# Two-pass up-projections on four PSUM banks, modulation sums on a new schedule, constants in two loads, and a few reorderings

## The reference, cut to what matters

```python
sh1, sc1, g1, sh2, sc2, g2 = split(silu(c) @ w_ada + b_ada, 6)      # w_ada: 2048 x 12288
h_l = rms_norm(x, norm1_w) * (1 + sc1) + sh1                        # h_c: the same for ctx
... = split(h_l @ w_in, IN_OFFSETS)                                 # gated linear + differential attention
gates = sigmoid(h_l @ w_gate + b_gate)
x = x + g1 * ((g_a * (ya @ w_proj_gla) + g_b * (yb @ w_proj_diff)) @ w_out)
h2 = rms_norm(x, norm2_w) * (1 + sc2) + sh2
u = h2 @ w_up                                                       # 2048 x 11264
u = sum(up[:, j:j + T] * conv_w[j] for j in range(3)) + conv_b      # a 3-tap conv over tokens
x = x + g2 * ((silu(gate) * val) @ w_down)                          # gate, val = halves of u
```

## Time and profile before

| | |
|---|---|
| median of 3 runs | 2309.18 us |
| the profiled execution | 2309.0 us, its span 2307.2 us |
| TensorE matmuls busy | 2235.6 us, 97% |
| TensorE weight loads busy (beside the matmuls) | 2007.1 us, 87% |
| VectorE busy | 1486.6 us, 64% |
| ScalarE busy | 1026.8 us, 45% |
| mean granted TensorE clock | 0.994 of full speed |

### The profile page before, as it was taken

One profiled execution on the slowest core, in us unless ns is written; L12 is line 12 of the kernel. 1 busy time (PEld: TensorE's weight loads), 2 busy tenths in 40 slices (PEclk: granted clock), 3 DMA queues, 4 the chain that ended last, 5 costly groups with the idle time before them and its releaser, 6 DMA issues.

```text
span 2307.2 us, 37356 instructions
## 1 busy us (share of the span) xinstructions
PE 2235.6 (97%) x15465; PEld 2007.1 (87%) x15465; DVE 1486.6 (64%) x2116; ACT 1026.8 (45%) x1410; POOL 52.7 (2%) x68
## 2 busy tenths in 40 slices
PE   5899999999999999999999999999999999999998
PEld 2577877999988999779999988999978998999986
DVE  2347866487576579777888854566675644576664
ACT  3134343354555633344444433444454434454443
POOL 3000000021000000000000000000000000000000
PEclk9999999999999999999999999999999999999999
DMA  9956766454444578866777655555555566534454
GB/s 364 379 163 208 250 191 216 132 148 137 139 135 129 186 248 287 284 236 203 229 245 258 226 190 192 183 183 183 183 178 194 171 189 200 171 129 137 129 199 148
DMA packets 249738, 458.75 MB, mean 199 GB/s; under 512 B 18995, under 2 KB 43889, under 8 KB 248160
## 3 DMA queue, kind: packets, MB, share of 16 engines
q1 hardware_dynamic: 246496, 442.47, 59.4%
q0 software_dynamic: 2496, 9.69, 1.2%
q10 hardware_dynamic: 576, 4.19, 0.5%
HBM read 454.20 MB, written 2.10 MB: 198 GB/s over the span
## 4 chain that ended last, share of the span: by engine, by line
PE 83%; DVE 7%; DMA 3%; DVEq 2%; ACT 2%; issue 1%; SPq 1%; ACTq 0%; POOLq 0%; POOL 0%
PE psum L660 74%; DVE fast L1919 2%; PE psum L637 2%; DVE sbuf L1973 1%; DMA sbuf<-in_w_ada 1%; DMA sbuf<-in_w_up 1%; ACT fast L1335 1%; PE psum L1169 1%; DVEq L1972 1%; PE psum L916 1%; PE psum L971 1%; DVE fast L1941 1%; PE psum L731 1%; PE psum L1199 1%; PE psum L990 1%
## 5 line engine op out<-in xcount | busy, mean ns | idle before, releaser
L660 PE MATMUL psum<-fast,fast 128*128 128x256 f32 (+1 forms) x13424 | 2028.1, 312 | 14.6 <-DVE fast L1919 12.4
L660 PEld LDWEIGHTS psum<-fast,fast 128*128 128x128 f32 x13424 | 1845.0, 190 | 186.6 <-issue 41.3
L1919 DVE TENSOR_TENSOR fast<-sbuf,fast 128x1024 fp32r<-128x1024 f32 (+5 forms) x685 | 784.1, 1153 | 661.9 <-ACT fast L1335 654.1
L1335 ACT ACTIVATE fast<-sbuf 128x1024 fp32r<-128x1024 f32 (+4 forms) x689 | 681.9, 997 | 1024.0 <-PE psum L660 882.8
L1973 DVE SCALAR_TENSOR_TENSOR sbuf<-sbuf,sbuf 128x512 f32<-128x512 f32 x210 | 157.9, 752 | 20.2 <-DMA sbuf<-in_w_ada 2.7
L1335 ACT ACTIVATE sbuf<-psum 128x512 f32<-128x512 f32 (+4 forms) x193 | 86.1, 469 | 93.6 <-PE psum L660 48.2
L637 PE MATMUL psum<-sbuf,sbuf 128*128 128x128 f32 (+2 forms) x349 | 59.2, 286 | 19.3 <-DMA sbuf<-in_consts 10.1
L637 PEld LDWEIGHTS psum<-sbuf,sbuf 128*128 128x128 f32 (+2 forms) x349 | 43.3, 147 | 30.1 <-DMA sbuf<-in_consts 10.1
L1941 DVE TENSOR_TENSOR fast<-sbuf,fast 128x512 fp32r<-128x512 f32 (+1 forms) x61 | 53.4, 876 | 4.9 <-issue 0.4
L1694 ACT ACTIVATE sbuf<-psum,sbuf 128x256 f32<-128x256 f32 x88 | 44.1, 551 | 0.0
L2354 DVE SCALAR_TENSOR_TENSOR sbuf<-psum,sbuf,sbuf 128x255 f32<-128x255 f32 x88 | 38.5, 479 | 3.3
(11 more groups left out here) (265 smaller groups left out, 956.5 us busy)
## 6 DMA issues: line engine op xcount, KB each, us to landing
sbuf<-in_w_ada SPq DMA_DIRECT2D x192, 512.0 KB, 5.1
sbuf<-in_w_up SPq DMA_DIRECT2D x176, 512.0 KB, 4.6
sbuf<-in_w_in SPq DMA_DIRECT2D x154, 512.0 KB, 3.7
sbuf<-in_w_down SPq DMA_DIRECT2D x88, 512.0 KB, 3.9
sbuf<-in_w_gate SPq DMA_DIRECT2D x64, 512.0 KB, 3.6
sbuf<-in_w_out SPq DMA_DIRECT2D x64, 512.0 KB, 4.8
sbuf<-in_w_proj_gla SPq DMA_DIRECT2D x16, 512.0 KB, 4.7
sbuf<-in_w_proj_diff SPq DMA_DIRECT2D x16, 512.0 KB, 6.2
```

The costliest lines, as they stand in the source:

```text
L660: last = mm(out, lhsT, rhs, start=first and key not in opened, stop=end, skip_group_check=True)
L1335: return A(out, in_, ACT.Copy, scale=scale)
L1919: last = tt(lo, raw, hi.bitcast(F32), ALU.subtract)
```

## The change

Up-projections: hi times [hi | lo] of the activations in one matmul of 512 columns (a whole bank), then lo times hi in 256 columns into its first half. A job takes four banks (gate 0 to 3, value 4 to 7). ScalarE copies the second halves out, VectorE adds them onto the first halves in PSUM, then `centre` and `taps` go on as before. Sums: block 16 and 17 move beside w_gate, 18 and 19 keep 16 sums beside pg, pd and out, 20 to 23 get fixed steps beside w_up. Constants: only `ones` and `rowsel` (132 columns) are loaded at the start, the other constants and w_a_up after block 7. The merges of a pd job move into the steps of the next job; in key_norms the side work goes ahead of rest and sums; some roundings go behind the copies out of PSUM; the rest after out3 goes behind row_variance. The compression stage's semaphores are joined under two names, with the same waits.

```diff
-          ("cmprel", 32), ("cmpmask", 32), ("levels", 7 * P), ("rowsel", 4),
+CONSTS = [("ident", 128), ("ones", 128), ("rowsel", 4), ("blk64", 128), ...
+NCONST0 = CCOL["blk64"][0]
+UP_SUMS = [16 * i + r for i in range(6) for r in (6, 7, 9, 12, 13, 15)][:32]
+for _i in range(KF // 4):
+    BANKS[f"ug{_i}"], BANKS[f"uv{_i}"] = (0, 1, 2, 3), (4, 5, 6, 7)
...
-        for n in range(8):
-            self.add(f"gate{n}", panel("w_gate", 512 * n, 512))
+        self.beside([(f"gate{n}", panel("w_gate", 512 * n, 512)) for n in range(8)], ada, (16, 17),
+                    [1 + 15 * n // 4 for n in range(16)], {})
...
-                    + [... "w_out" ...], ada, range(16, 20), 15, 8)
+                    + [... "w_out" ...], ada, (18, 19),
+                    [6 + 2 * n for n in range(8)] + [31 + 3 * n for n in range(8)], {4: 16, 8: 17, 24: 18, 56: 19})
-        self.beside(ups[:KFA // 2], ada, range(20, 24), 5, 2, 14)
+        self.beside(ups[:KFA // 2], ada, range(20, 24), UP_SUMS, {36: 20, 52: 21, 68: 22, 100: 23})
...  # POOL
-            pool.dma_start(cst[:, P:], dram["consts"][:, P:NCONST1]).then_inc(S("consts_loaded"), 16)
+            pool.dma_start(cst[:, P:NCONST0], dram["consts"][:, P:NCONST0]).then_inc(S("consts_loaded"), 16)
...
+            pool.wait_ge(S("plain_multiplied"), st.done("ada7")[1])
...  # the eight w_a_up loads
+            pool.dma_start(cst[:, NCONST0:], dram["consts"][:, NCONST0:NCONST1]).then_inc(S("consts_loaded"), 16)
...  # TensorE
+            def wide(first, act):
+                def products(k, hi, lo):
+                    return [(2 * b, cut(bank(b), 2, T),
+                             [(hi[:, m * P:(m + 1) * P], act[:, :, k, :]),
+                              (lo[:, m * P:(m + 1) * P], act[:, 0, k, :], bank(b, 0, T))])
+                            for m, b in enumerate(range(first, first + 4))]
...
-                    gemm(f"u{'gv'[v]}{i}", features(v, hL), ...)
+                    gemm(f"u{'gv'[v]}{i}", wide(4 * v, XR[:, 0, :, :, :]), ...)
...  # ScalarE, at step 8 (gate) and 0 (value) of 16; centre one step later
+            def copy_halves(s, i):
+                for b in range(2):
+                    copy(ftap[s][:, 2 * b:2 * b + 2, :], cut(banks(4 * s + 2 * b), 2, 2, T)[:, :, 1, :]
+                         ).then_inc(S("halves_copied"), 1)
...  # VectorE, same steps; taps one step later
+            def halves(s, i):
+                for b in range(2):
+                    dve.wait_ge(S("halves_copied"), 4 * i + 2 * s + b + 1)
+                    pair = cut(banks(4 * s + 2 * b), 2, 2, T)
+                    tt(pair[:, :, 0, :], pair[:, :, 0, :], ftap[s][:, 2 * b:2 * b + 2, :], ALU.add).then_inc(S("halves_added"), 1)
...
             for name in ("dk1", "dv0", "dv1"):
-                steps(name)
+                for g in st.job[name]:
+                    next(side, None)
+                    rest_chunk(st.nth[g] + 2)
+                    modulation(st.nth[g])
...
+            for n in range(4):
+                steps(f"pd{n}")
+                side = merges(n)
...
             row_variance(48, 4, ("x1_squared", 8))
+            rest_chunk(st.nth[st.job["out3"][-1]] + 2)
```

More of the change, by code:

```diff
@@ L249, in add, with beside @@
             self.counts[kind] += 1
-    def beside(self, jobs, ada, parts, num, den, first=0):
+    def beside(self, jobs, ada, parts, steps, folds=None):
         todo = [(a, i) for a in parts for i in range(len(ada[a]))]
-        at = {}
-        for n, x in enumerate(todo):
-            at.setdefault(first + n * num // den, []).append(x)
+        at, base = {}, self.counts[0]
+        for x, step in zip(todo, steps, strict=True):
+            at.setdefault(step, []).append(x)
+        for step, a in (folds or {}).items():
+            self.fold_at[base + step] = self.keep_at[base + step + 1] = a
         for n, (name, c) in enumerate((name, c) for name, chunks in jobs for c in chunks):
@@ L280, in before, with folded_before @@
             tiles += len(BANKS[job]) - 1
+    def folded_before(self, s):
+        return [a for step, a in self.fold_at.items() if a >= 20 and step < s]
     def landed(self, g):
@@ L1495, in _ @@
             for j in range(2):
[L1496 removed]
+                steps(f"dk{j}", j)
                 if j == 0:
@@ L2280, in _, with merges @@
                         ).then_inc(emptied, 1)
-            for n in range(4):
-                steps(f"pd{n}")
+            def merges(n):
                 for b in range(2):
```

111 lines of the change are left out of this document (68 added, 43 removed).

## The result

The changed kernel takes 2294.82 us, the median of 4 runs (2292.72 to 2296.4), against 2308.96 before on the same chip: ratio 0.9938, 95% interval 0.9925 to 0.9951. That is faster by 14.1 us, inside the stated range of 2268 to 2296, where 30.8 were forecast. The profiled execution took 2294.8 us, its span is 2292.6 (before 2307.2).

The account below looks back on a forecast made before the run. TensorE, busy 97% of the span, was taken to bound the kernel. From 2309.0 us, the terms -18.3 + 3.0 - 9.2 - 3.2 - 3.1 = -30.8 gave 2278.2 us, with a stated range of 2268 to 2296.

Parts of the forecast that it names:

- Step 1: w_up: one 512-column pass replaces two of 256, 346.4 ns a pair against 359.4, over 1408 pairs: -18.3 us.
- Step 2: First 96 chunks of w_up: added copies and adds make VectorE late, 0.5 us per group: +3.0 us, bounds 0 and 10.0.
- Rival A: First 96 chunks of w_up: VectorE sets the pace, nothing is left of 768 pairs' gain; 2285.2 us, chance 0.17.
- the last sentence of the prediction: Beside w_up: the forecast fails if VectorE is over 95% taken and TensorE's windows fall under 98%.
- Step 3: pd and out: sums moved away and merges spread remove TensorE's stops and low clock: -9.2 us, bounds -6 and -9.7.
- The sums beside w_gate: w_gate: the 16 sums moved there fit VectorE's free time and do not delay the attention: 0 us.
- Rival C: w_gate: the sums placed there delay the attention, 14 us exposed; 2292 us, chance 0.08.
- Step 4: Start: 1.21 MB of constants and w_a_up leave the stretch with saturated DMA: -3.2 us, bounds 0 and -4.5.
- Step 5: Key stage: key scaling ahead of rest and sums, and an earlier copy out of PSUM: -3.1 us, bounds 0 and -3.1.
- Rival B: w_up: time goes with columns, not with matmuls, so two passes gain 0; 2293.5 us, chance 0.07.

Follow-up runs that it names:

- the groups: The changed kernel with each w_up chunk doing its 8 passes of 512 columns first, then its 8 of 256: 2295.52 us, ratio 0.9940.
- merges_back: The changed kernel with both halves of a pd job's merges done at once after it, as before the change: 2301.52 us, ratio 0.9966.
- sums_back_beside_out: The changed kernel with the sums of blocks 16 and 17 back beside the projections and w_out, none beside w_gate: 2300.76 us, ratio 0.9966.

## Why the prediction was right and wrong

**Step 1, two passes for three (-18.3): the size of the term failed.** The two paces that it was built of were right, each among its like: 226.7 and 120.0 ns inside the groups. What the step overlooked is that it put them side by side: it added the pair up to 346.4 ns, and the pair took 353.3 in all of the last 80 chunks and much of the first 96. A change of size costs 10 ns on average between groups of eight; the alternation has two steady states, 353.3 and 346.7 ns a pair. The first gives 6.1 ns a pair (8.6 us in all), the second 12.7, nearly the forecast's 13.0. The last 80 chunks ran wholly in the slow state: 4.3 us gained where 8.3 were forecast. The earlier trace rows held a warning, that 512 columns took 226.6 in one place and 231.3 in another; I took the nearer row and left 231.3 as a bound. With it the step gives -11.7, still more than came. The price from the Trainium skill's "TensorE: Matmul & The Clock Gate", section "Back-to-back issue gap", gives 3.5 us for the step, nearer to what came, but not by its figures: it has 109.2 and 215.8 ns for the two sizes, and the groups ran at 120.0 and 226.7. That section also calls the formula the gap of a single matmul by itself, so the prediction stretched it when it set it against a stream.

**Step 2, VectorE (+3.0): direction right, size too small.** The step named the mechanism, lateness of rests and slots freed late, and put 0.5 us on each group. In the first 96 chunks the intervals between matmuls that are longer than their pace, other than at folds and at the first chunks, add up to 7.2 us in the changed kernel and to nothing in that with the sums spread: 7.2 us of stops, inside the stated bound of 10.0. Rival A's outcome came, that nothing is left of those 768 pairs (282.1 us with two passes, 281.8 with three). Its condition, no spare time on VectorE, did not: counted as the prediction counts it, VectorE was taken for 164.8 of 180 us (92%, before 87%), since each stop is made by one bad sequence and not by the mean. Of the two conditions in the last sentence of the prediction one came true: TensorE's windows beside w_up fell under 98% (76.85 us of 80 from 1160 to 1240, 96%), while VectorE stayed under 95%.

**Step 3, sums and merges (-9.2): right, -11.7,** of which 1.7 are two folds that only moved ahead of pd0, so -10.0. The sums brought most of it, the merges 2.9.

**The sums beside w_gate (0): wrong by 4.7 us,** 6.4 less the 1.7 of the two folds. The cover was counted from where exponentials end to where TensorE needs them, 4.1 us against 1.8. That was one step of sixteen, and sixteen steps don't have the same cover: where a sum stood in a step with a maximum, TensorE came to wait 0.3 to 1.5 us. Rival C named the mechanism with a chance of 0.08; its price of 14 us was three times too high. Putting the attention first brings back 2.4 of the 4.7; 1.6 of what is left are the two stops that remain, and why these remain was not looked into.

**Step 4, late constants (-3.2): right in sign, -5.4** in this pair of profiles, past the stated bound of -4.5; -4.2 in the middle of all profiles with late constants, which is inside it. In 20 to 60 us, with the DMA engines at 1.05 in both, TensorE was busy 31.1 us with the constants early and 35.3 late, at clock 1.00; behind it, to 125 us, the mean clock was 0.89 and 0.92. How much of what exceeds the 3.2 is the clock's, no run separates.

**Step 5, keys first (-3.1): right, -3.2** from gv0 to gq.

**Not in the prediction: downb, +3.3.** Nothing of the change touches it. But w_up now ends with ScalarE's and VectorE's last tap work a step later, and an order that had cost 1.7 us costs 2.6, after which the clock fell in this execution and in seven other profiles, but not in four. The forecast looked for stops only where the edits were.

In sum, by the table: 8.8 us are missing in w_up (4.8 and 4.0, from pace and stops, less the 2.5 that are won there without the passes), 6.4 from w_gate on, 3.3 in downb and 2.5 in the first w_down part and the second layer, against 4.8 more than forecast at the start and in pd and out: 16.2. The folds shift 1.7 us between w_gate and pd and 0.9 between w_up and w_down within this sum. That the total came inside the range is in part luck: steps 3 and 4 gave more than forecast while step 1 gave half of its term in w_up's last 80 chunks and, less the stops of step 2, nothing in the first 96. Rival B gave 2293.5, near the result, by a mechanism that the groups refute: time does go with matmuls.

## What to carry to other kernels

A pace measured in a run of equal matmuls holds for runs of equal matmuls; before two sizes are mixed, measure the mix, and where a mix is needed, group the sizes or look for a steady state that an interruption can set. A second engine that is busy 87% of a stretch has no free time to count on: place its extra work by how many long steps follow one another, over the longest stretch in which its result isn't needed yet. When an edit gains nothing by the total, read its stages, and first count what work has moved from one to another: here two folds made a stage look 1.7 us worse than it was, the wide passes won 4.3 us and lost 4.9 behind it, and once the other places were mended they brought 11 to 13. One profile of each kernel doesn't settle a stage that scatters, such as the start.

## What the runs showed of the hardware

- Alternating matmuls of 512 and 256 columns run steadily at 353.3 or 346.7 ns a pair, for hundreds of pairs; folds (a 128x512 fp32 matmul between two chunks) left 346.7 behind them in the stretches read, stops by a late rest left either. What the state is stays open.
- In groups of eight, the first five matmuls of 512 columns behind 256s took 233, 236, 229, 232 and 231 ns before they settled at 226.7; the first two of 256 behind 512s took 113 and 119 before they settled at 120.0.
- A stop of 3.15 us was followed by matmuls at the lower clock level, and so was the wait of 5.24 us for the normed rows (128 columns 214 ns apart, 109 elsewhere). Stops of 0.80, 1.68, 1.92 (merges_back) and 2.44 us (sums_back_beside_out) were not. Stops of 2.62 to 2.64 us at one place of downb were in eight profiles (512 columns 427 ns apart) and were not in four; 36 matmuls behind them took 10.18 and 8.60 us.
- 512 columns with activations as weights took 226.7 ns in most of w_out and a cycle of 226.7, 232.7 and 234.0 in w_down, in every kernel; not explained.
